# Seven feed-forward stages of a two-block transformer stack: one pair of weight blocks of the down projection as seven block products instead of eight, two of the weight sums made by adding transfers

## The reference

```
D_MODEL = 1024; SEQ = 256; D_FF = 2816

def swiglu(x, w_gate, w_up, w_down):
    return (jax.nn.silu(x @ w_gate) * (x @ w_up)) @ w_down
...
for l in range(DEPTH):
    x = x + 0.5 * swiglu(rmsnorm(x, ffn1_norm[l]), ffn1_w_gate[l], ffn1_w_up[l], ffn1_w_down[l])
    h = rmsnorm(x, mix_norm[l])
    x = x + hybrid_mixer(h, ...)
    x = x + 0.5 * swiglu(rmsnorm(x, ffn2_norm[l]), ffn2_w_gate[l], ffn2_w_up[l], ffn2_w_down[l])
```

## Time and profile before

| | |
|---|---|
| median of 3 runs | 2436.91 us (2436.86 to 2438.19) |
| profiled execution | 2436.97 us, of which the profile's span is 2435.2 us |
| PE busy | 2407.2 us, 99% of the span |
| DVE busy | 1710.7 us, 70% |
| ACT busy | 1255.4 us, 52% |
| POOL busy | 205.5 us, 8% |
| granted tensor clock | 0.999 of full |
| moved by DMA | 504.42 MB, mean 207 GB/s |

### The profile page before, as it was taken

The page is one execution under the profiler, slowest core; times in us unless marked ns, Lnnn a source line. Parts: engine busy times, 40 slices in busy tenths (PEclk is TensorE's granted clock), DMA queues, the critical chain, the costliest instruction groups (busy, mean ns, idle before and its releaser), DMA issues.

```text
span 2435.2 us, 30841 instructions
## 1 busy us (share of the span) xinstructions
PE 2407.2 (99%) x12606; PEld 2053.7 (84%) x12606; DVE 1710.7 (70%) x1755; ACT 1255.4 (52%) x1367; POOL 205.5 (8%) x358
## 2 busy tenths in 40 slices
PE   8999999999999999999999999999999999999998
PEld 6889998888889988888889878888888898778887
DVE  6555867857866778768658657777687677577884
ACT  5435545535537545445435664555455356645552
POOL 0100200101100100100100010001001000100010
PEclk9999999999999999999999999999999999999999
DMA  8765445856754446856864445468568544454672
GB/s 333 238 216 191 157 154 209 276 202 214 275 202 182 162 158 225 277 203 226 272 215 175 163 151 212 169 224 280 201 211 276 186 182 156 151 197 170 220 272 105
DMA packets 82549, 504.42 MB, mean 207 GB/s; under 512 B 11609, under 2 KB 12761, under 8 KB 30185
## 3 DMA queue, kind: packets, MB, share of 16 engines
q1 hardware_dynamic: 61488, 433.23, 49.4%
q0 software_dynamic: 19744, 67.65, 8.7%
q10 hardware_dynamic: 1176, 1.58, 0.4%
HBM read 476.72 MB, written 25.69 MB: 206 GB/s over the span
## 4 chain that ended last, share of the span: by engine, by line
PE 91%; DVE 5%; ACT 3%; issue 1%; DMA 1%; SPq 0%; POOL 0%; DVEq 0%; POOLq 0%; ACTq 0%
PE acc L709 23%; PE acc L711 22%; PE acc L710 22%; PE acc L677 4%; PE acc L678 4%; PE acc L679 4%; DVE w_lo L576 2%; PE aux L810 1%; PE aux L812 1%; PE aux L811 1%; PE aux L944 1%; ACT w_hi L568 1%; DMA raw<-in_w 1%; ACT tmp L1689 1%; PE bc L810 1%
## 5 line engine op out<-in xcount | busy, mean ns | idle before, releaser
L576 DVE TENSOR_TENSOR w_lo<-raw,w_hi 128x2048 fp32r<-128x2048 f32 (+1 forms) x438 | 978.7, 2245 | 489.1 <-ACT w_hi L568 487.9
L568 ACT ACTIVATE w_hi<-raw 128x2048 fp32r<-128x2048 f32 (+1 forms) x438 | 822.2, 1882 | 551.7 <-PE acc L711 387.6
L709 PE MATMUL acc<-w_hi,x_hi 128*128 128x512 f32 (+1 forms) x1624 | 633.4, 390 | 3.6 <-DVE x_lo L1941 2.1
L711 PE MATMUL acc<-w_lo,x_hi 128*128 128x512 f32 (+1 forms) x1624 | 628.5, 387 | 0.0
L710 PE MATMUL acc<-w_hi,x_lo 128*128 128x512 f32 (+1 forms) x1624 | 628.4, 387 | 0.0
L709 PEld LDWEIGHTS acc<-w_hi,x_hi 128*128 128x128 f32 x1624 | 305.0, 188 | 69.4 <-issue 6.1
L711 PEld LDWEIGHTS acc<-w_lo,x_hi 128*128 128x128 f32 x1624 | 305.0, 188 | 62.9
L710 PEld LDWEIGHTS acc<-w_hi,x_lo 128*128 128x128 f32 x1624 | 305.1, 188 | 61.7 <-issue 1.0
L709 PE MATMUL acc<-w_hi,h_parts 128*128 128x512 f32 x704 | 274.5, 390 | 0.0
L711 PE MATMUL acc<-w_lo,h_parts 128*128 128x512 f32 x704 | 274.0, 389 | 0.0
L710 PE MATMUL acc<-w_hi,h_parts 128*128 128x512 f32 x704 | 273.9, 389 | 0.0
(11 more groups left out here) (435 smaller groups left out, 2729.0 us busy)
## 6 DMA issues: line engine op xcount, KB each, us to landing
raw<-in_w SPq DMA_DIRECT2D x399, 1024.0 KB, 4.9
squares<-tmp POOLq DMA_DIRECT2D x40, 512.0 KB, 3.3
tmp<-squares POOLq DMA_DIRECT2D x160, 128.0 KB, 4.4
raw<-in_w SPq DMA_DIRECT2D x18, 512.0 KB, 4.8
tmp<-in_norm_gb POOLq DMA_DIRECT2D x8, 1024.0 KB, 5.9
tmp<-in_norm_gb POOLq DMA_DIRECT2D x6, 512.0 KB, 3.7
tmp<-in_gate_rows POOLq DMA_DIRECT2D x12, 256.0 KB, 2.9
squares<-tmp POOLq DMA_DIRECT2D x8, 256.0 KB, 2.8
```

Source lines behind the costliest of these rows:

```text
L568: nc.scalar.activation(w_hi[:, slot, 0:kind], raw[:, slots[c], 0:kind], ACT.Copy).then_inc(hi_done, 1)
L576: nc.vector.tensor_tensor(w_lo[:, slot, 0:kind], raw[:, slots[c], 0:kind], w_hi[:, slot, 0:kind].bitcast(F32), ALU.subtract).then_inc(lo_d ...
L709: nc.tensor.matmul(out, vh, wh, start=first and k == 0, stop=False)
L711: last = nc.tensor.matmul(out, vh, wl, start=False, stop=last_k and k == nk - 1)
```

## The change

In s = 2, 3, 5, 6, 9, 10 and 13, the first two hidden groups (blocks k = 0 to 7) times both column halves of w_down, 8 block products before, become seven. The stage has 15 places in the stream instead of 12:

| place from d | name | what | matmuls |
|---|---|---|---|
| 0 | D_FIRST | plain chunk, hidden group 2, n = 0, both tt | 24 |
| 1 | D_T1 | D12 loaded, D11 added to it by a transfer; product into `bc` | 12 |
| 2 | D_B11 | D11; product into `aux` bank 1 | 12 |
| 3 | D_B22 | D22; product into output tile (1, 0) | 12 |
| 4 | D_THREE | plain, hidden group 3, n = 0 | 24 |
| 5 | D_T2 | sum on DVE; product added onto B11's in `aux` bank 1 | 12 |
| 6 | D_FOUR | plain, hidden group 4, n = 0 | 24 |
| 7 | D_T3 | difference on DVE; product onto the same bank | 12 |
| 8 | D_B21 | D21; product into tile (0, 0) | 12 |
| 9, 10 | D_HALF0, D_HALF1 | plain halves, hidden group 5 | 12, 12 |
| 11, 12 | D_TWO, D_LAST2 | plain, n = 1, tt = 0 first, later tt = 1 | 24, 24 |
| 13 | D_LAST | plain, n = 1, tt = 0, and tt = 1 as the very last | 24 |
| 14 | D_T4 | T2 with D21 added by a transfer; product into tile (1, 1), before D_LAST's tt = 1 | 12 |

The core of the diff follows. `ffn0` keeps the old order; what is left out renames semaphores and counts. `down_group` with `plain`, and `into` (twelve matmuls like `product`, but into an output tile), are PE's; `hsum_high` and the list behind it are ACT's; `norm`, `h_sums` (called in `group` behind `hid_low(1)`), `hsum_low`, `x_add` and `down` are DVE's; `grow` and the loop behind it are POOL's.

```diff
+D11, D21, D12, D22 = 0, 1, 6, 7
+DOWN = (2, D12, D11, D22, 3, None, 4, None, D21, 0, 1, 8, 9, 10, None)
+DOWN_SLOT_OF = {D_FOUR: 3, D_T3: 5, D_HALF0: 3, D_HALF1: 3, D_TWO: 3, D_LAST2: 3, D_LAST: 3, D_T4: 9}
+DOWN_ADD = {D_T1: D11, D_T4: D21}
...
-                for last in (c + 24, c + 30, c + 36):
+                for last in (c + 24, c + 39, c + 39):
                     self.block(last)
...
         def split_hi(act, c, slot, kind):
             if c in sums:
                 act.wait_ge(weight_sum, sums.index(c) + 1)
+            elif c in grown:
+                act.wait_ge(weight_added, 16 * (grown.index(c) + 1))
...
+                def down_group(d, b, tile):
...
+                    def plain(c, n, k0, nk, first, last_k, tts=(0, 1), done=1):
+                        chunk_ready(c)
+                        for tt in tts:
+                            tl = tile + 2 * n + tt
+                            if first and (n == 0 or tt):
+                                bank_free(tl)
+                            pe.wait_ge(hid_parts, 12 * f + 2 * (k0 // 4) + tt + 1)
+                            last = tokens(c, tl, tt, h_hi, h_lo, k0, nk, first and (n == 0 or tt == 1), last_k and (n == 1 or tt == 0))
+                            if tt:
+                                if done:
+                                    last.then_inc(chunk_done, done)
+                            elif last_k:
+                                last.then_inc(tile_done, 1)
...
+                    plain(d + D_FIRST, 0, 8, 4, True, False)
+                    pe.wait_ge(sum_parts, 8 * b + 5)
+                    pe.wait_ge(outs_ready, 3 * b + 1)
+                    product(d + D_T1, e_, *s1, True)
+                    pe.wait_ge(kept_silu, 2 * b + 2)
+                    product(d + D_B11, b_, *h11, True)
+                    pe.wait_ge(sum_parts, 8 * b + 7)
+                    bank_free(tile + 2)
+                    into(d + D_B22, tile + 2, *s4, True, False)
+                    plain(d + D_THREE, 0, 12, 4, False, False)
+                    pe.wait_ge(x_added, 6 * b + 3)
+                    product(d + D_T2, b_, *s2, False)
+                    plain(d + D_FOUR, 0, 16, 4, False, False)
+                    pe.wait_ge(sum_parts, 8 * b + 8)
+                    pe.wait_ge(x_added, 6 * b + 4)
+                    product(d + D_T3, b_, *s3, False)
+                    into(d + D_B21, tile, *h12, False, False)
...
+                    plain(d + D_LAST, 1, 16, 4, False, True, (0,))
+                    plain(d + D_TWO, 1, 8, 4, False, False, (1,))
+                    plain(d + D_LAST2, 1, 12, 4, False, False, (1,))
+                    into(d + D_T4, tile + 1, *h22, False, True, 0)
+                    if parts(s + 1):
+                        x_turn(s + 1, 0)
+                    plain(d + D_LAST, 1, 16, 4, False, True, (1,), 2)
...
+                def hsum_high(q):
+                    act.wait_ge(sum_ready, 8 * (f - 1) + 4 + q + 1)
+                    nc.scalar.activation(HSUM_HI[q], HQ4[q].rearrange("p k a j -> p k (a j)"), ACT.Copy).then_inc(sum_hi, 1)
...
+                if s:
+                    d = c0 + DOWN_AT
+                    ahead.to(d + 2)
+                    hid_high(3)
+                    ended_chunk(act, d - 1)
+                    hsum_high(0)
+                    silu(5, 0)
+                    silu(5, 1)
+                    hsum_high(1)
+                    hsum_high(2)
+                    ahead.to(d + 3)
+                    hsum_high(3)
+                    choose_sqrt()
+                    ahead.to(d + 4)
+                    hid_high(4)
+                    ahead.to(d + 8)
+                    hid_high(5)
...
             def norm(N):
...
-                if not early:
+                if not early or s:
                     add_out(s, 0, 1)
                 add_out(s, 1, 1)
...
+                def h_sums(b):
+
+                    (h11, h12), (h21, h22) = ((landed(0, tt), landed(1, tt)) for tt in range(2))
+                    s1, s2, s4, s3 = HQ4
+                    dve.wait_ge(hid_landed, 64 * (6 * f + 2))
+                    V_.tensor_tensor(s1, h21, h22, ALU.subtract).then_inc(sum_ready, 1)
+                    dve.wait_ge(sum_ready, 8 * b + 5)
+                    V_.tensor_tensor(s2, s1, h11, ALU.subtract).then_inc(sum_ready, 1)
+                    dve.wait_ge(sum_ready, 8 * b + 6)
+                    V_.tensor_tensor(s4, h12, s2, ALU.add).then_inc(sum_ready, 1)
+                    V_.tensor_tensor(s3, h11, h21, ALU.subtract).then_inc(sum_ready, 1)
+
+                def hsum_low(q):
+                    dve.wait_ge(sum_hi, 8 * (f - 1) + 4 + q + 1)
+                    V_.tensor_tensor(HSUM_LO[q], HQ4[q].rearrange("p k a j -> p k (a j)"), HSUM_HI[q].bitcast(F32),
+                                     ALU.subtract).then_inc(sum_parts, 1)
...
+                def x_add(c, bank, n, tt, sign):
+
+                    xs = x[:, tt, 512 * n:512 * n + 512]
+                    ended_chunk(dve, c)
+                    V_.scalar_tensor_tensor(xs, bank, sign * weight_of(s), xs, ALU.mult, ALU.add).then_inc(x_added, 1)
+
+                def down(d, b):
+
+                    b_, e_ = aux[:, 1, :], bc[:, :]
+                    ahead.to(d + 2)
+                    hid_low(3)
+                    hsum_low(0)
+                    ahead.to(d + 3)
+                    dve.wait_ge(lo_done, d + D_T1 + 1)
+                    landed_chunk(d + D_B22)
+                    V_.tensor_tensor(weights(d + D_T2), weights(d + D_T1), weights(d + D_B22), ALU.add).then_inc(weight_sum, 1)
+                    times(5, 0)
+                    times(5, 1)
+                    turn_squares(5)
+                    hsum_low(1)
+                    hsum_low(2)
+                    ahead.to(d + 4)
+                    hid_low(4)
+                    hsum_low(3)
+                    dve.wait_ge(lo_done, d + D_B11 + 1)
+                    dve.wait_ge(weight_sum, sums.index(d + D_T2) + 1)
+                    V_.tensor_tensor(weights(d + D_T3), weights(d + D_T2), weights(d + D_B11), ALU.subtract).then_inc(weight_sum, 1)
+                    ahead.to(d + 5)
+                    x_add(d + D_T1, e_, 1, 0, 1.0)
+                    x_add(d + D_T1, e_, 1, 1, 1.0)
+                    x_add(d + D_B11, b_, 0, 0, 1.0)
+                    ahead.to(d + 8)
+                    hid_low(5)
+                    dve.wait_ge(x_added, 6 * b + 2)
+                    x_add(d + D_T2, b_, 1, 0, -1.0)
+                    ahead.to(d + 11)
+                    x_add(d + D_T3, b_, 0, 1, 1.0)
+                    x_add(d + D_T3, b_, 1, 1, -1.0)
+                    ahead.to(d + 13)
+                    dve.wait_ge(x_added, 6 * b + 6)
+                    add_out(s, 0, 0)
+                    ahead.to(base[s + 1] - 1)
...
+            def grow(c):
...
+                pool.dma_start(raw[:, slots[c], 0:WIDE], t[f"w{WIDE}"][more[c]], accum_op=ALU.add).then_inc(weight_added, 16)
...
                     for i in range(6):
+                        if s and i == 2:
+                            pool.wait_ge(sum_ready, 8 * f)
+                        if s and i == 5:
+                            pool.wait_ge(sum_parts, 8 * f)
+                            load_norm(s + 1)
                         permute(f, i)
+                        if s and i == 2:
+                            grow(base[s] + DOWN_AT + D_T1)
+                    if s:
+                        grow(base[s] + DOWN_AT + D_T4)
```

119 lines of the change are left out of this document (89 added, 30 removed).

## The result

The changed kernel takes **2529.68 us** (median of three runs, 2523.24 to 2531.2) against 2436.91: a ratio of 1.0372, interval 1.0344 to 1.0401, and 92.8 us slower. (The ratio goes by the means of the runs and comes to 90.7 us; the 92.8 is the difference of the medians.) Forecast were 2463 us and a range from 2438 to 2480. The direction and most of the places were right, the size was not. The profiled execution took 2529.68 us too. First the waits of PE: us in total, times, longest.

What follows compares the result with a forecast made beforehand. PE, busy 99% of the span, was taken as the bound, its matmul count setting the time while DVE delivers. -19.0 + 7 x 3.4 + 21.1 = +26 on 2436.97 gave 2463 us; own range 2452 to 2475, wider 2438 to 2480.

Steps and rivals of the forecast that it cites:

- Removed, 19.0 us: One product of twelve matmuls gone from each of seven down stages, 2.72 us each, 19.0 us in all.
- Hidden sums at no cost: The four hidden sums on DVE, 2.4 us in the gate/up stage, fit into 9 us to spare and cost nothing.
- In-stage waits of 1.1 and 2.3 us: Each down stage: PE waits 1.1 us ahead of B22 and 2.3 ahead of T2's product, 3.4 per stage.
- The walk through DVE's list: Stepping through DVE's fixed instruction order in stage s = 2, which put each stage 0.7 us longer.
- Boundary, 3.0 and 3.6 us: Between stages, ahead of x_turn(s + 1, 1): waits of 3.0 or 3.6 us; with 1.3 at the end, 21.1 together.
- Adding transfer, 5.9 to 11.8 us, cost nothing: T1's adding transfer on POOL takes 5.9 to 11.8 us; being 2.5 us late is hidden by DVE's idle time.
- The margin of T4's transfer: T4's adding transfer has over 15 us of room.
- "I find no further wait" behind T2: Rest of the down stage: PE's seven twelves against DVE's five splits, two of them halves, bring no further wait.
- The clock falls, 6%: Rival: twelve slower matmuls after each of 13 waits over 2 us, 31 us more, 2494 us; chance 6%.
- 8 for group 5: Part of the prediction's own range: up to 8 us from hidden group 5's work, with the norm's load ahead in POOL's queue.

Runs made afterwards that it cites:

- pause3: Kernel before the change with PE pausing for three successive POOL memsets ahead of the fourth chunk in each of seven down stages: 2471.6 us, ratio 1.0138.
- b_hid3: boundary with hidden group 3's hi copied by ACT behind B22's split and its lo by DVE behind hsum_low(2): 2488.6 us, ratio 1.0213.
- boundary: Changed kernel with D_LAST's second token half ahead of T4's product, chunk_done released earlier, add_out(1, 1) before add_out(0, 1): 2500.2 us, ratio 1.0259.
- b_all: boundary plus hidden group 3 behind B22's split, both sums by DVE instead of adding transfers, and bias_store late: 2474.4 us, ratio 1.0160.
- t1plain: Changed kernel with T1's adding transfer overwriting instead of adding, so T1 holds D11's weights alone: 2513.5 us, ratio 1.0317.
- b_t4x: b_all with DVE and ACT lists reordered, T4's sum by adding transfer again, and bias_store behind the next sub-layer's norm: 2466.2 us, ratio 1.0127.
- b_swap: b_all with lists reordered, B21 ahead of T3, other raw slots for D_HALF1 and D_TWO, bias_store behind the next norm: 2445.0 us, ratio 1.0033.
- b_biaslate: boundary with bias_store of s = 6 issued behind the stage's last split, at the end of ACT's list: 2502.1 us, ratio 1.0270.
- pause1: Kernel before the change with PE pausing for one POOL memset ahead of the fourth chunk in each of seven down stages: 2446.5 us, ratio 1.0039.
- the best version: b_swap with T2's sum and hsum_low(0) moved ahead of B22's split in DVE's list: 2442.6 us, ratio 1.0019.

## Why the prediction was wrong, step by step

Two steps failed most. The prediction held that waits of at most 3.6 us would not bring the lower clock, and it walked every stage as if hidden group 3 were out of ACT's way when the stage starts, with the adding transfer at a cost of nothing. The runs show the lower clock behind a wait of 3.09 us alone (pause3), and waits ahead of B22 of 25.4 us in sum that fall to 7.4 when group 3 leaves the head of ACT's list (b_hid3 against boundary's 25.9). The steps in order:

- *Removed, 19.0 us.* Right in size, by the twelve matmuls at 0.227 us.
- *Hidden sums at no cost.* Nothing in the runs speaks against it; no run tests it alone.
- *In-stage waits of 1.1 and 2.3 us.* The walk through DVE's list was close for the case that it described: b_all shows 0.82 (1.40 in s = 6) and 2.25 to 2.27. In the changed kernel they were 3.5 and 1.75 (s = 2), 25.4 us for B22 in seven stages instead of 7.7. The walk had group 3 done before the stage's start, as in s = 2; in four of the seven stages before the change it was not, and by 2.9 us or more in three of them.
- *Boundary, 3.0 and 3.6 us.* The place, the mechanism and the waits were right (2.52 and 3.64). I took the wait to be the whole cost; boundary gave back 29.4 us where I had 21.1.
- *Adding transfer, 5.9 to 11.8 us, cost nothing.* The length was right (10.6 in the median, 8.6 to 12.5). This is a step that failed: I asked only when T1 would be late, and not what stands behind the transfer on its engine. Group 3's store and reads did, and group 3 headed ACT's list. t1plain puts the adding of T1 at 13 to 16 us and b_hid3 the place in the list at 12, each with its clock drops. The margin of T4's transfer was gone too (b_t4x against b_swap, 21 us, though they differ in order too). By the Trainium skill (DMA: Bandwidth & Descriptors, Queues, rings and completion order) each DMA engine goes round its queues packet by packet, so transfers share the engines. The 10.6 us beside the loads fit that; no run here shows the sharing itself.
- *"I find no further wait" behind T2.* Wrong: 21.2 us at plain chunks, 11.3 of them in the one wait of s = 6. I read them as loads that compete with T4's sum (b_t4x) and, in s = 6, with bias_store (b_biaslate); how much each takes is not separated. The store's 38 us of transfer were in the profile of before, where ACT had slack for it; I did not ask what it does when the slack goes. That stage is 17 us longer than the mean of the other six.
- *The clock falls, 6%.* The step that failed most plainly. I had the price (12 x 0.2 = 2.4 us a time; 1.5 to 1.8 measured on average) and dismissed it because my waits were at most 3.6 us while the one in the trace was 9.0. pause3 shows it at 3.09 us, where pause1 at 1.07 us shows nothing of it. About 19 us in the changed kernel.
- The restarts, 0.27 us behind each wait however short, I did not count: 10 us. My expectations for the pauses had 0.16 and were a little low for it: pause1 took 9.6 us, 1.37 per stage.

Of the 67 us between 2463 and 2529.7, then, 19 are the clock, 10 the restarts, 29 more waiting than the 44.9 us forecast (7 x 3.4 + 21.1; 73.5 measured: 17.7 more at B22, 21.2 at plain chunks, 12.6 less at T2, which the others hid, and small ones), and 9 not assigned. In the best version the gaps are still 6.8 us longer; 4.9 of that are the waits of about 0.25 and 1.37 us at x_turn(s + 1, 1) that boundary left. What stays open is why single stages differ by up to 3 us between kernels whose edits don't touch them.

The sum of the stated range was not right either: 7 x 1, 6 x 0.7 and 8 for group 5 give 2482 as its upper end, where the prediction wrote 2475. It makes no difference to the outcome.

## What to carry to other kernels

Where one engine has been busy without a gap, price a wait by what follows it as well: here a wait of 1.1 us cost 1.4, one of 3.1 us cost 5.0. When a transfer is added to a queue, walk that queue: what stands behind it, and at the head of whose list its result is waited for. A stage that stands for seven has to be compared with the other six first: s = 2 had its group 3 ready early, four others had not. And averages of busy time say whether a change can fit, not whether it does: the same products and sums in other orders, slots and places of issue gave 2474 and 2443 us.

## What the runs showed of the hardware

- In fourteen kernels (the changed one and all others but the two with pauses), of PE's waits ahead of a 512-wide matmul, none of 310 between 0.23 and 1.6 us was followed by the lower clock; of 46 between 1.6 and 2.3 us 16 were, with 1.5 us lost behind each on average, and of 62 over 2.3 us 59, with 1.8 (the other three were of 2.8, 2.8 and 3.5 us, the last the one ahead of B22 in s = 2 shown above). The lower level shows as a matmul every 0.43 us instead of 0.227, at a granted clock of 0.50. The Trainium skill (TensorE: Matmul & The Clock Gate, What's actually happening) has two levels, 1.2 and 2.4 GHz, and the windows' 0.50 and 1.00 agree.
- A transfer of 1 MB that adds to its destination took 10.6 us (median of 14) where SP's plain ones took 4.9 and the one from POOL in t1plain (s = 2) 6.4, and 0.95 us of POOL to issue instead of 0.57.
- A store of 1.5 MB in pieces of 1.5 KB took 38 us beside the loads before the change, 43 after it and 36 to 43 in the others in which its end can be read, and moving it within the stage or to its end saved nothing that can be told from the spread; issued behind the next norm (b_swap) it delayed nothing that PE waited for by over 1 us.
